# A one-core trunk layer on Trainium2: places of its own for the first half of a second operand set, a new order of vector work, one square on another engine, a last product over three steps

## The chip, the cores and the metric

The kernel runs on one NeuronCore of one Trainium2 chip. The metric is device time in microseconds (us). Engines: PE (TensorE, matrix products), DVE (VectorE), ACT (ScalarE), POOL (GpSimd), SP (SyncE, which issues DMAs), and 16 DMA engines. Each engine takes its own instructions strictly in program order; semaphores order one engine against another.

## The reference

One layer, with x of 1024 x 2048 and all in float32:

```python
hn = rmsnorm(x, norm_w)
proj = hn @ w_in                      # (1024, 2048) @ (2048, 6400)
q, k, v, g_attn, h, c_gate, b_gate, g_conv = split(proj)
attn = windowed attention(q, k, v)    # 16 query heads, 2 kv heads, bias, sinks
conv = b_gate * causal_conv3(c_gate * h)
mixed = concat(attn * silu(g_attn), conv * silu(g_conv))
x = x + mixed @ w_out                 # (1024, 2048) @ (2048, 2048)
return rmsnorm(x, final_norm_w)
```

## The kernel before

**Products.** The float32 products are made from halves: every operand is split into a high part (rounded to the type fp32r, by an ACT copy) and a low part (what is left, by a DVE subtraction), and a product is three matmuls (high x high, high x low, low x high). Each pair of 2 x 2 blocks is multiplied by Strassen's method in Winograd's form, so there are seven products per block (named 1 to 7 by `p`), each over 8 slices of the inner dimension, taken two slices to a step: four steps a product, 28 steps a block of output columns (`LEN`), eight blocks (`BLOCKS`: GATES, QKV, four convolution blocks, OUT0, OUT1), 224 steps in all (`STEPS`). A step is four output tiles (five in block QKV) of 6 matmuls each. The order of the products in block GATES is 2, 1, 3, 6, 7, 5, 4: steps 0 to 3 are product 2, steps 4 to 7 product 1, steps 8 to 11 product 3, and so on.

**What feeds a step n.** `w_hi(n)` (ACT, L947) and `w_lo(n)` (DVE, L1293) split two slices of weights from `raw` into a ring of three places. In the blocks GATES and OUT0 (`ON_CHIP`), `x_hi(l)` (ACT, L973) and `x_lo(l)` (DVE, L1301), l = 2n and 2n+1, split the activation side from `z` into five places of `x_main`; POOL then stores the halves to the DRAM tensor `x_park` (`store_x`, L488), and the blocks that follow load them from there (`load_x`, SP, L546). A place of `x_main` can be written again when its step is done and its store has landed. Some products take sums of blocks: `s1` to `s4` (DVE, L1355, L1361, L1373, L1367) make them in `raw` for weights, `t1` to `t4` in `z` for activations. `w_hi` of steps 8 to 11 waits for `s4`.

**The first block.** The input x arrives untransposed. PE turns it: first the left half (`turn_x0`, L1826), then, once ACT has scaled it by the row norms (`scale_x_lo`, `scale_x_hi`, L995, L999), the right half (`turn_x1`, L1862). DVE takes turned slices 0 to 7 of the right half straight into `t1` (`t1_from_turn`, L1332); ACT copies slices 8 to 15 (`place_1`, L1005). The first tile of step 8 waits for all eight copies (`wait_bank`). The row norms of the left half come from eight ACT squares (`square_x0`, L982), three small POOL operations (`x_inv_std`), a PE product that spreads them (`turn_factors`, L1842) and a DVE copy (L1656).

**Parking.** Steps 0 to 3 (product 2) ran on activations without the norm factor, so their halves are not the ones that later blocks need. `b21` (DVE, L1340) multiplies `z[:, 0, 8:16]` by the factors in place, `park_hi` (ACT) and `park_lo` (DVE, L1347) split each of its 8 slices again, and `store_park` (POOL, L845, L847) stores both halves, 16 stores of 256 KB. The loads of steps 28 to 31 wait until all have landed; the places of step 28's load (`x_far0`) are also read until step 25.

**What orders the work.** Nothing plans it: each engine walks over the steps and the four quarters of each step, and tables such as `T1_AT[(step, quarter)]` say what is put in at that point of the engine's own queue. A position is an order, not a time; time is set by the waits. Within a quarter DVE takes: sums of finished tiles, `place_0`, `x_lo`, `w_lo`, `t1_from_turn`, `s1` and so on, in the order of the code. ACT takes `x_hi`, `w_hi`, squares, scalings, `place_1`, `park_hi`.

**The end.** The last `TAIL` steps are done tile by tile: tile 0 over these steps, then tile 1, and so on. After each tile DVE subtracts it into `e`, ACT squares it, DVE and POOL make the norm, and ACT and DVE scale the rows and ACT and SP store them.

Of the kernel before, what the change touches and what calls it, by code (L numbers as in the profile page):

```python
# [9 lines left out]
ALU = mybir.AluOpType  # L10
# [56 lines left out]
XH = 5  # L67
TAIL = 2

# [93 lines left out]
def _slots():  # L163
    holder, loads, stores = {}, {}, {}
    for n in range(STEPS):
# [12 lines left out]
        else:  # L178
# [3 lines left out]
            for j in places:  # L182
# [33 lines left out]
W_LO_AT = {(1, 0): 2, (2, 1): 3, (2, 3): 4}  # L216
X_HI_AT = {(1, 0): (4,), (1, 1): (5,), (1, 3): (6,), (2, 0): (7,), (3, 2): (8, 9), (4, 0): (10,),
           (4, 1): (11,), (4, 3): (12,), (5, 0): (13,), (5, 1): (14,), (6, 0): (15,), (7, 1): (16,), (7, 2): (17,),
           (7, 3): (18,)}
X_LO_AT = {(1, 0): (4,), (1, 1): (5,), (1, 3): (6,), (2, 0): (7,), (3, 2): (8, 9), (4, 0): (10,),  # L220
           (4, 2): (11,), (4, 3): (12,), (5, 0): (13,), (5, 1): (14,), (6, 0): (15,), (7, 1): (16,), (7, 2): (17,),
           (7, 3): (18,)}
# [22 lines left out]
def build(nc, x, norm_w, w_in, sinks, conv_w, conv_b, w_out, rel_bias, final_norm_w, one_hot, out):  # L245
    ctx = ExitStack()
    with ctx:
# [38 lines left out]
        x_tile[7] = [place[:, 1, k:k + 2, :].rearrange("p a c -> p (a c)") for place, k in ((z, 4), (raw, 14))]  # L286
        square = z[:, 1, 0:2, :].rearrange("p a c -> p (a c)")
        setup_rows = scratch[0:(TAPS + 1) * GROUPS + KT, 0:P]
# [206 lines left out]
        def _(sp):  # L495
# [31 lines left out]
            def load_x(n):  # L527

                b, p, q = place(n)
                made = GATES if b < OUT0 else OUT0  # L530
                for was, i in X_BEFORE[n, 0]:
                    sp.wait_ge(step_done, was + 1)
                    if was // LEN in ON_CHIP:
                        sp.wait_ge(x_stored[was // LEN == OUT0][S_TURN[was, i][0]], S_TURN[was, i][1])
                if x_pair(n) > 1 and n - (made + 1) * LEN < 2:

                    sp.wait_ge(x_lo_ready, x_index(at(made, 4, QP - 1 if x_pair(n) == 3 else 1), 1) + 1)
                for i in range(2):
                    if is_parted(at(made, p, q)):
                        sp.wait_ge(park_stored, 16 * 2 * HK)  # L540
# [283 lines left out]
        def _(pool):  # L824
# [7 lines left out]
            def x_inv_std(tiles, turn):  # L832

                pool.wait_ge(x_squared, 8 + 2 * turn)
                pool.tensor_tensor(x_var[:, tiles], x_ssq[:, tiles], x_ssq_lo[:, tiles], ALU.add).then_inc(x_var_ready, 1)
                pool.wait_ge(x_var_ready, 2 * turn + 1)
                pool.tensor_scalar(x_var[:, tiles], x_var[:, tiles], 1.0 / D, EPS, ALU.mult, ALU.add
                                   ).then_inc(x_var_ready, 1)
                pool.wait_ge(x_var_ready, 2 * turn + 2)
                pool.tensor_tensor(x_rstd[:, tiles], x_var[:, tiles], minus_half[:, 0:tiles.stop - tiles.start], ALU.pow  # L840
                                   ).then_inc(x_rstd_ready, 1)

            def store_park(j):
                pool.wait_ge(park_hi_ready, j + 1)
                pool.dma_start(x_park[0, j // 2, :, j % 2, 0:N], z[:, 1, j, :]).then_inc(park_stored, 16)  # L845
                pool.wait_ge(park_lo_ready, j + 1)
                pool.dma_start(x_park[0, j // 2, :, j % 2, N:], z[:, 0, HK + j, :]).then_inc(park_stored, 16)  # L847
# [82 lines left out]
        def _(act):  # L930
# [54 lines left out]
            def square_x(t):  # L985
                i = TILES1.index(t)
                act.wait_ge(x_part_loaded[(1, 2, 0, 5)[t - 4]], 32 if t == 7 else 48)
                for c in range(2):
                    act.wait_ge(x_squared, 8 + 2 * i + c)
                    act.activation(square, x_tile[t][c], ACT.Square,  # L990
                                   accum_out=(x_ssq if c else x_ssq_lo)[:, t:t + 1]).then_inc(x_squared, 1)
# [16 lines left out]
            def park_hi(j):  # L1008

                act.wait_ge(b21_ready, j // 2 + 1)  # L1010
                act.wait_ge(x_lo_ready, x_index(at(GATES, 5, j // 2), j % 2) + 1)
                act.activation(z[:, 1, j, :].bitcast(F32R), z[:, 0, HK + j, :], ACT.Copy).then_inc(park_hi_ready, 1)

            def copy_out(b, p, t):

                to = (0, 2, 3)[COPIED[b].index(p)]
                if t == 0:
# [21 lines left out]
                    else:  # L1039
                        if b == GATES:  # L1040
                            act.wait_ge(x1_turned, KT)
                        elif b == QKV:
# [13 lines left out]
            def tanh_gate(i, half):  # L1056
# [4 lines left out]
                if i > 0:  # L1061
                    act.wait_ge(gate_stored[0], 16)
                else:
                    act.wait_ge(x1_turned, KT)
                if i > 1:
# [4 lines left out]
            def more_hi(p):  # L1070
                i = AT[QKV][p]
                c, h = W_HOME[p]
                if i == 0:

                    act.wait_ge(x_lo_ready, 2 * LEN)
                    act.wait_ge(park_stored, 16 * 2 * HK)
                if p == 2:
# [104 lines left out]
            for n in range(STEPS):  # L1182
                b, p, q = place(n)
                i = AT[b][p]
                for quarter in range(4):
# [23 lines left out]
                    if quarter == 0:  # L1209
                        l = 2 * n + 3  # L1210
                        if X_TABLED <= l < 2 * STEPS and l // (2 * LEN) in ON_CHIP:
                            x_hi(l // 2, l % 2)
                        if 5 <= n + 2 < STEPS:
                            w_hi(n + 2)
# [43 lines left out]
                    if b == OUT1:  # L1258
# [19 lines left out]
            square_y(20, 3, 0)  # L1278
            for t in range(4):
                if t < 3:  # L1280
                    square_y(21 + t, 3, t + 1)
                scale_back(0, t)
                store_back(0, t)
# [3 lines left out]
        def _(dve):  # L1287
# [16 lines left out]
            def place_0(k):  # L1304
# [38 lines left out]
            def park_lo(j):  # L1343

                dve.wait_ge(park_hi_ready, j + 1)
                dve.wait_ge(t4_ready, j // 2 + 1)
                dve.tensor_tensor(z[:, 0, HK + j, :].bitcast(F32R), z[:, 0, HK + j, :], z[:, 1, j, :], ALU.subtract  # L1347
                                  ).then_inc(park_lo_ready, 1)
# [293 lines left out]
            for n in range(STEPS):  # L1642
                b, p, q = place(n)
                i = AT[b][p]
                for quarter in range(4):
# [18 lines left out]
                    if (n, quarter) in W_LO_AT:  # L1664
                        w_lo(W_LO_AT[n, quarter])
                    if quarter == 0:
                        l = 2 * n + 3
# [14 lines left out]
                    if quarter == 1:  # L1682
                        if 5 <= n + 2 < STEPS:
                            w_lo(n + 2)
# [3 lines left out]
                    if b == GATES:  # L1688
                        for k in T1_AT.get((n, quarter), ()):
                            t1_from_turn(k)  # L1690
                        if quarter == 0 and 5 <= n < 9:
                            s1(GATES, n - 5)
                        if (n, quarter) in B21_AT:
# [5 lines left out]
                    if quarter == 2:  # L1699

                        if 5 <= n < 9:
                            s2(GATES, n - 5)
                            s4(GATES, n - 5)
                        wb, wp, wq = place(n + 2) if n + 2 < STEPS else (BLOCKS, 0, 0)
# [97 lines left out]
            for t in range(4):  # L1802
                sums(OUT1, 4, t)
                if t > 0:
                    finish_0(t - 1)
                y_variance(4 + t)
            finish_0(3)


        @block.tensor  # L1810
        def _(pe):
# [227 lines left out]
```

## Time and profile before

| | |
|---|---|
| median of 3 runs | 1361.8 us (1359.88 to 1362.35) |
| the profiled execution's own time | 1360.45 us |
| its span, first to last instruction | 1358.6 us |
| PE busy | 1335.0 us, 98% |
| DVE, ACT, POOL busy | 919.3, 538.6, 93.3 us |
| DMA over the span | 287 GB/s |

The times in rows are from the first instruction; about 1.85 us of the execution's own time lie outside the span. A row of a timeline gives start, duration, engine, line, operation, tiles out and in, shape and count, and in brackets how long the engine had been idle before it and what ended that. Ends of matmuls are modelled: the next matmul can start before the row's end.

### The profile page before, as it was taken

The numbers are of one execution on the slowest core, as the hardware profiler recorded it, in microseconds if no ns is written. First come the engines' busy times: TensorE is split into PE (matmuls) and PEld (weight loads), VectorE is DVE, ScalarE is ACT, GpSimd is POOL, SyncE is SP. The second block draws the span as 40 slices with busy tenths as digits, with TensorE's granted clock in tenths as the row PEclk, the third lists the DMA queues.
The fourth block names the chain that finished last, engine by engine and source line by source line (L and its number), as shares of the span: only waits on it lengthen the run. The fifth ranks groups of instructions, "written<-read, shape, count | busy, mean of one in ns | idle before, by whom it ended". The sixth has DMA issues, their size and how long they took to land.

```text
span 1358.6 us, 16600 instructions
## 1 busy us (share of the span) xinstructions
PE 1335.0 (98%) x6034; PEld 1102.0 (81%) x6034; DVE 919.3 (68%) x1141; ACT 538.6 (40%) x941; POOL 93.3 (7%) x158
## 2 busy tenths in 40 slices
PE   9899999999999999999999999999999999999997
PEld 7688878888887888888888888878888788888886
DVE  5888976423467557985589845898439896666376
ACT  6754532322233443434334343343423444421454
POOL 0211411000000000000000000000000221200001
PEclk9999999999999999999999999999999999999999
DMA  9766995988978999969999699987988888899777
GB/s 327 293 233 248 398 411 198 285 298 283 336 246 274 278 292 309 260 215 284 286 290 281 199 316 289 294 252 218 297 315 319 322 269 278 280 317 358 281 253 305
DMA packets 206432, 390.02 MB, mean 287 GB/s; under 512 B 78912, under 2 KB 129168, under 8 KB 184720
## 3 DMA queue, kind: packets, MB, share of 16 engines
q1 hardware_dynamic: 186768, 321.83, 72.4%
q0 software_dynamic: 18368, 62.92, 12.6%
q10 hardware_dynamic: 1216, 4.21, 0.8%
q8 instruction: 48, 0.79, 0.2%
q14 instruction: 32, 0.26, 0.1%
HBM read 294.18 MB, written 98.93 MB: 289 GB/s over the span
## 4 chain that ended last, share of the span: by engine, by line
PE 87%; DVE 5%; DMA 4%; issue 2%; ACT 1%; SPq 0%; POOL 0%; DVEq 0%; ACTq 0%; POOLq 0%
PE banks L1902 82%; DMA x_far<-x_park 1%; DMA x_park<-z 1%; PE banks L1925 1%; PE banks L1937 1%; DMA qkv_park<-e 1%; DVE w_ring L1293 1%; PE banks L1946 1%; DVE x_main L1301 1%; PE banks L1947 1%; DVE raw L1355 0%; PE banks L1826 0%; DVE e L1444 0%; DVE z L1400 0%; DMA raw<-in_w_in_dram 0%
## 5 line engine op out<-in xcount | busy, mean ns | idle before, releaser
L1902 PE MATMUL banks<-x_main,w_ring 128*128 128x512 f32 x2352 | 552.4, 392 | 0.4 <-ACT x_main L973 0.2
L1902 PEld LDWEIGHTS banks<-x_main,w_ring 128*128 128x128 f32 x2352 | 438.8, 188 | 90.8 <-issue 1.1
L947 ACT ACTIVATE w_ring<-raw 128x1024 fp32r<-128x1024 f32 x224 | 236.4, 1056 | 550.4 <-PE banks L1902 539.2
L1293 DVE TENSOR_TENSOR w_ring<-raw,w_ring 128x1024 fp32r<-128x1024 f32 x224 | 274.2, 1224 | 218.8 <-ACT w_ring L947 218.7
L1902 PE MATMUL banks<-x_far,w_ring 128*128 128x512 f32 x1680 | 395.2, 392 | 3.9 <-DMA x_far<-x_park 3.8
L1902 PEld LDWEIGHTS banks<-x_far,w_ring 128*128 128x128 f32 x1680 | 314.0, 188 | 69.5 <-issue 4.4
L1902 PE MATMUL banks<-w_ring,x_main 128*128 128x512 f32 x1008 | 230.0, 389 | 0.8 <-DVE x_main L1301 0.8
L1902 PEld LDWEIGHTS banks<-w_ring,x_main 128*128 128x128 f32 x1008 | 189.1, 188 | 40.5 <-issue 1.2
L488 POOL DMA_DIRECT2D x_park<-x_main x104 | 56.1, 540 | 1019.3 <-DVE x_main L1301 1014.5
L973 ACT ACTIVATE x_main<-z 128x512 fp32r<-128x512 f32 x112 | 69.8, 624 | 136.7 <-issue 94.5
L1301 DVE TENSOR_TENSOR x_main<-z,x_main 128x512 fp32r<-128x512 f32 x112 | 76.8, 688 | 47.6 <-ACT x_main L973 47.5
L1902 PE MATMUL banks<-w_ring,x_far 128*128 128x512 f32 x336 | 77.4, 389 | 0.1
L1902 PEld LDWEIGHTS banks<-w_ring,x_far 128*128 128x128 f32 x336 | 63.0, 188 | 13.5 <-issue 0.5
L1054 ACT ACTIVATE e<-banks 128x512 f32<-128x512 f32 x92 | 54.7, 597 | 46.3 <-PE banks L1902 45.8
L1107 ACT ACTIVATE probs<-logits,small 128x129 f32<-128x129 f32 x128 | 50.0, 393 | 47.1 <-DVE small L1510 47.0
L1498 DVE SCALAR_TENSOR_TENSOR logits<-banks,bias 128x512 f32<-128x512 f32 (+1 forms) x32 | 21.5, 672 | 45.8 <-PE banks L1925 45.8
L1361 DVE TENSOR_TENSOR raw<-raw 128x1024 f32<-128x1024 f32 x32 | 41.2, 1288 | 1.1
L1367 DVE TENSOR_TENSOR raw<-raw 128x1024 f32<-128x1024 f32 x32 | 39.2, 1224 | 2.9
L1373 DVE TENSOR_TENSOR raw<-raw 128x1024 f32<-128x1024 f32 x32 | 39.1, 1221 | 0.4
L1355 DVE TENSOR_TENSOR raw<-raw 128x1024 f32<-128x1024 f32 x32 | 39.0, 1218 | 0.0
L1434 DVE TENSOR_TENSOR e<-e,banks 128x512 f32<-128x512 f32 x24 | 16.4, 685 | 27.6 <-PE banks L1902 14.3
L1423 DVE TENSOR_TENSOR e<-e,banks 128x512 f32<-128x512 f32 x32 | 21.4, 684 | 19.0 <-PE banks L1902 18.9
(143 smaller groups left out, 855.1 us busy)
## 6 DMA issues: line engine op xcount, KB each, us to landing
x_far<-x_park SPq DMA_DIRECT2D x84, 1024.0 KB, 7.2
x_main<-x_park SPq DMA_DIRECT2D x84, 1024.0 KB, 7.1
x_park<-x_main POOLq DMA_DIRECT2D x104, 512.0 KB, 5.4
raw<-in_w_in_dram SPq DMA_DIRECT2D x128, 256.0 KB, 5.3
raw<-in_w_in_dram SPq DMA_DIRECT2D x32, 512.0 KB, 11.1
raw<-in_w_out_dram SPq DMA_DIRECT2D x32, 512.0 KB, 6.0
q_cur<-qkv_park SPq DMA_DIRECT2D x64, 128.0 KB, 5.5
z<-mix_park SPq DMA_DIRECT2D x16, 512.0 KB, 8.0
```

The costliest lines, as they stand in the source:

```text
L488: engine.dma_start(x_park[0 if n < LEN else 1, n % LEN, :, i, :], x_main[:, k, :, :].rearrange("p a c -> p (a c)").bitcast(F32)).then_inc( ...
L947: act.activation(w_ring[:, n % NW, :, 0, :], raw[:, c, k:k + 2, :], ACT.Copy).then_inc(w_hi_ready, 1)
L973: act.activation(x_halves(n)[i][:, 0, :], z[:, h, kt16, :], ACT.Copy).then_inc(x_hi_ready, 1)
L1054: act.activation(e_tile(b, to, t), banks[:, BANK[b, p, t], :], ACT.Copy).then_inc(copy_ready, 1)
L1107: op = act.activation(probs[:, j, :], logits[u % 2][:, j, :], ACT.Exp, bias=row_min[:, j:j + 1], scale=-1.0, accum_out=row_sum[:, j:j + 1])
L1293: dve.tensor_tensor(w_ring[:, n % NW, :, 1, :], raw[:, c, k:k + 2, :], w_ring[:, n % NW, :, 0, :], ALU.subtract).then_inc(w_lo_ready, 1)
L1301: dve.tensor_tensor(half[:, 1, :], z[:, h, k * HK + 2 * q + i, :], half[:, 0, :], ALU.subtract).then_inc(x_lo_ready, 1)
L1355: dve.tensor_tensor(raw[:, 1, k, :], raw[:, 1, k, :], raw[:, 1, high, :], ALU.add).then_inc(s1_ready, 1)
L1361: dve.tensor_tensor(raw[:, 0, k, :], raw[:, 1, k, :], raw[:, 0, k, :], ALU.subtract).then_inc(s2_ready, 1)
L1367: dve.tensor_tensor(raw[:, 0, high, :], raw[:, 0, high, :], raw[:, 0, k, :], ALU.subtract).then_inc(s4_ready, 1)
L1373: dve.tensor_tensor(raw[:, 0, k, :], raw[:, 1, high, :], raw[:, 0, k, :], ALU.subtract).then_inc(s3_ready, 1)
L1902: op = pe.matmul(bank, left, right, start=(first and i == 0), stop=(kt == HK - 1 and i == 2), skip_group_check=goes_on)
```

## The change

- `b21(0)` and `b21(1)` move from steps 16 and 17 to steps 10 and 13. The second splitting of slices 0 to 3 moves from steps 19 and 20 to steps 11, 15 and 16. It writes both halves into parts of `e` that are free then (`park_stage`), and POOL stores both with one DMA of 512 KB (4 stores in place of 8). ACT's first tanh waits for two of them, ACT's copies of product 7 for all four. The waits for 16 stores become waits for the 12.
- `s2`, `s4` of the first weight sums move from quarter (5, 2) to (6, 1), behind the first four `t1_from_turn`; the others from (6, 2), (7, 2) to (7, 1), (7, 3); `s1(1)` from (6, 0) to (7, 0), `s1(2)` from (7, 0) to (7, 2).
- `w_hi(7)` moves from (5, 0) to (5, 2), `w_hi(8)` from (6, 0) to (6, 1), `w_hi(9)` from (7, 0) to (7, 2), `w_lo(7)` from (5, 1) to (5, 3), `w_lo(8)` from (6, 1) to (7, 0), `w_lo(9)` from (7, 1) to (7, 3), `x_hi` and `x_lo` of l = 15 from (6, 0) to (5, 3). The four `scale_x_hi` move from (5, 2), (5, 3) to (6, 0).
- The square of row tile 3's low half goes from ACT to DVE, as a product and a reduction.
- `TAIL` is 3; a step's operands are waited for where its first tile uses them; DVE's `finish_0(t)` comes right behind `y_variance(4 + t)`, and ACT's squares at the end no longer run one tile ahead.

```diff
-TAIL = 2
+TAIL = 3
-              (2, 0): ((0, 0), (0, 1)), (2, 1): ((0, 2), (0, 3))}
+              (2, 0): ((0, 0), (0, 1)), (2, 1): ((0, 2),)}
+SQUARED_BY_DVE = (2, 2)
-SCALE_HI_AT = {(5, 2): (7, 4), (5, 3): (5, 6)}
+SCALE_HI_AT = {(6, 0): (7, 4, 5, 6)}
-W_HI_AT = {(1, 0): 2, (2, 0): 3, (2, 3): 4}
-W_LO_AT = {(1, 0): 2, (2, 1): 3, (2, 3): 4}
+W_HI_AT = {(1, 0): 2, (2, 0): 3, (2, 3): 4, (3, 0): 5, (4, 0): 6, (5, 2): 7, (6, 1): 8, (7, 2): 9}
+W_LO_AT = {(1, 0): 2, (2, 1): 3, (2, 3): 4, (3, 1): 5, (4, 1): 6, (5, 3): 7, (7, 0): 8, (7, 3): 9}
+W_TABLED = 10
+S1_AT = {(5, 0): 0, (7, 0): 1, (7, 2): 2, (8, 0): 3}
+S24_AT = {(6, 1): 0, (7, 1): 1, (7, 3): 2, (8, 2): 3}
-B21_AT = {(16, 3): 0, (17, 3): 1, (18, 3): 2, (19, 3): 3}
-PARK_AT = {(19 + j // 2, 1 + 2 * (j % 2)): j for j in range(HK)}
+B21_AT = {(10, 3): 0, (13, 3): 1, (18, 3): 2, (19, 3): 3}
+PARK_AT = {(11, 1): 0, (11, 3): 1, (15, 1): 2, (16, 1): 3, (21, 1): 4, (21, 3): 5, (22, 1): 6, (22, 3): 7}
+STAGED = 4
...
+        park_stage = [e[:, i, 2 * j:2 * j + 2, :] for i in (1, 3) for j in range(2)]
...
             def store_park(j):
+                if j < STAGED:
+                    if j == 2:
+                        pool.wait_ge(park_stored, 16 * 2)
+                    pool.wait_ge(park_lo_ready, j + 1)
+                    pool.dma_start(x_park[0, j // 2, :, j % 2, :], park_stage[j].rearrange("p a c -> p (a c)")
+                                   ).then_inc(park_stored, 16)
+                    return
+                if j == STAGED:
+                    pool.wait_ge(park_stored, 16 * STAGED)
...
+            def square_last_low():
+
+                for i in (3, 4):
+                    dve.wait_ge(x_part_loaded[i], 16)
+                dve.tensor_tensor(squares, x_cols[0][:, 3, :], x_cols[0][:, 3, :], ALU.mult).then_inc(cols_ready, 1)
+                dve.wait_ge(cols_ready, 3)
+                dve.tensor_reduce(x_ssq_lo[:, 3:4], squares, AX_X, ALU.add).then_inc(cols_ready, 1)
...
-            for n in range(STEPS - TAIL, STEPS):
-                wait_operands(n)
             for t in range(4):
                 for n in range(STEPS - TAIL, STEPS):
                     q = place(n)[2]
+                    if t == 0:
+                        wait_operands(n)
```

## Rows read from the trace of the kernel before

**Rows 1.** The page, busy time of the engines.
```profile
PE 1335.0 (98%) x6034; PEld 1102.0 (81%) x6034; DVE 919.3 (68%) x1141; ACT 538.6 (40%) x941; POOL 93.3 (7%) x158
```

**Rows 2.** Timeline of PE alone, first 200 us.
```profile
32.02 1.16 PE L1842 MATMUL banks<-ident,small 128*128 128x128 f32 x8 [1.11 <-POOL small L840]
...
44.29 0.63 PE L1826 MATMUL banks<-ident,z 128*128 128x128 f32 x4 [0.98 <-DVE z L1313]
...
53.20 0.55 PE L1862 MATMUL banks<-ident,e 128*128 128x128 f32 x3 [0.98 <-ACT e L995]
...
59.27 0.55 PE L1862 MATMUL banks<-ident,e 128*128 128x128 f32 x3 [1.36 <-DVE z L1332]
...
66.73 0.67 PE L1862 MATMUL banks<-ident,e 128*128 128x128 f32 x3 [2.08 <-DVE z L1332]
...
74.56 110.67 PE L1902 MATMUL banks<-x_main,w_ring 128*128 128x512 f32 x487
...
188.72 7.33 PE L1902 MATMUL banks<-x_far,w_ring 128*128 128x512 f32 x24 [2.37 <-DMA x_far<-x_park]
```

**Rows 3.** Windows: length, busy of PE, PEld, DVE, ACT, POOL, granted clock, DMA.
```profile
68.00:70.00 2.00, 2.00 (x8) 1.61 (x7) 1.69 (x2) 1.60 (x3) 0.00 (x0) 0.50 0.00 0
...
190.00:192.00 2.00, 2.00 (x6) 1.56 (x5) 2.00 (x4) 0.00 (x0) 0.00 (x0) 0.50 1.06 384
```

**Rows 4.** Timeline of ACT, the last of the eight squares of the left half.
```profile
29.05 1.06 ACT L982 ACTIVATE z<-z 128x1024 f32<-128x1024 f32 x1
```

**Rows 5.** Groups by shape on DVE: busy us, mean ns.
```profile
L1510 DVE TENSOR_REDUCE small<-logits 128x4 f32<-128x516 f32 x32 | 22.1, 691 | 1.1
```

**Rows 6.** Timeline of DVE, steps 2 to 7.
```profile
31.18 1.23 DVE L1293 TENSOR_TENSOR w_ring<-raw,w_ring 128x1024 fp32r<-128x1024 f32 x1 [4.55 <-ACT w_ring L947]
...
53.88 1.22 DVE L1361 TENSOR_TENSOR raw<-raw 128x1024 f32<-128x1024 f32 x1
55.20 1.23 DVE L1367 TENSOR_TENSOR raw<-raw 128x1024 f32<-128x1024 f32 x1
57.86 0.69 DVE L1301 TENSOR_TENSOR x_main<-z,x_main 128x512 fp32r<-128x512 f32 x1 [1.43 <-ACT x_main L973]
58.47 2.72 DVE L1332 SCALAR_TENSOR_TENSOR z<-banks,cols,z 128x512 f32<-128x512 f32 x4
```

**Rows 7.** Timeline of ACT, steps 5 to 7.
```profile
49.50 1.04 ACT L947 ACTIVATE w_ring<-raw 128x1024 fp32r<-128x1024 f32 x1
...
65.95 1.06 ACT L947 ACTIVATE w_ring<-raw 128x1024 fp32r<-128x1024 f32 x1 [7.18 <-DVE raw L1367]
...
75.13 1.26 ACT L1005 ACTIVATE z<-banks,cols 128x512 f32<-128x512 f32 x2
```

**Rows 8.** Chain of waits, 155 to 200 us.
```profile
159.98 14.92 DMA x_park<-z
...
174.98 13.64 DMA x_far<-x_park
```

**Rows 9.** DMA queues (packets, MB, share) and issues (to landing), 142 to 162 us.
```profile
q0 software_dynamic: 1540, 5.37, 66.0%
...
raw<-in_w_in_dram SPq DMA_DIRECT2D x4, 512.0 KB, 21.8
```

**Rows 10.** Timelines of ACT, DVE and POOL before step 28.
```profile
178.86 0.63 ACT L973 ACTIVATE x_main<-z 128x512 fp32r<-128x512 f32 x1 [1.25 <-DMA x_park<-x_main]
...
181.62 3.44 DVE L1451 SCALAR_TENSOR_TENSOR e<-e 128x1024 f32<-128x1024 f32 x1
...
187.25 1.21 DVE L1458 TENSOR_TENSOR xw<-x_raw,xw 128x1024 fp32r<-128x1024 f32 x1
...
181.07 2.91 POOL L855 TENSOR_TENSOR x_raw<-x_raw 128x1024 f32<-128x1024 f32 x1
```

**Rows 11.** Timeline of all engines, the end.
```profile
1350.01 0.69 DVE L1444 TENSOR_TENSOR e<-e,banks 128x512 f32<-128x512 f32 x1 [0.72 <-PE banks L1902]
...
1352.96 1.15 ACT L1161 ACTIVATE raw<-raw,small 128x1024 f32<-128x1024 f32 x1 [0.47 <-POOL small L883]
```

More of the change, by code:

```diff
@@ L286, in build @@
         x_tile[7] = [place[:, 1, k:k + 2, :].rearrange("p a c -> p (a c)") for place, k in ((z, 4), (raw, 14))]
-        square = z[:, 1, 0:2, :].rearrange("p a c -> p (a c)")
+        square, squares = (z[:, 1, k:k + 2, :].rearrange("p a c -> p (a c)") for k in (0, 2))
+        park_stage = [e[:, i, 2 * j:2 * j + 2, :] for i in (1, 3) for j in range(2)]
         setup_rows = scratch[0:(TAPS + 1) * GROUPS + KT, 0:P]
@@ L539, in load_x @@
                     if is_parted(at(made, p, q)):
-                        sp.wait_ge(park_stored, 16 * 2 * HK)
+                        sp.wait_ge(park_stored, 16 * (2 * HK - STAGED))
                     else:
@@ L832, in x_inv_std @@
             def x_inv_std(tiles, turn):
-                pool.wait_ge(x_squared, 8 + 2 * turn)
+                pool.wait_ge(x_squared, 7 + 2 * turn)
+                pool.wait_ge(cols_ready, 4)
                 pool.tensor_tensor(x_var[:, tiles], x_ssq[:, tiles], x_ssq_lo[:, tiles], ALU.add).then_inc(x_var_ready, 1)
@@ L988, in square_x @@
                 for c in range(2):
-                    act.wait_ge(x_squared, 8 + 2 * i + c)
+                    act.wait_ge(x_squared, 7 + 2 * i + c)
                     act.activation(square, x_tile[t][c], ACT.Square,
@@ L1010, in park_hi @@
                 act.wait_ge(b21_ready, j // 2 + 1)
+                if j < STAGED:
+                    act.wait_ge(x1_turned, KT)
+                    act.activation(park_stage[j][:, 0, :].bitcast(F32R), z[:, 0, HK + j, :], ACT.Copy
+                                   ).then_inc(park_hi_ready, 1)
+                    return
                 act.wait_ge(x_lo_ready, x_index(at(GATES, 5, j // 2), j % 2) + 1)
@@ L1040, in copy_out @@
                         if b == GATES:
-                            act.wait_ge(x1_turned, KT)
+                            act.wait_ge(park_stored, 16 * STAGED)
                         elif b == QKV:
@@ L1063, in tanh_gate @@
                 else:
-                    act.wait_ge(x1_turned, KT)
+                    act.wait_ge(park_stored, 16 * 2)
                 if i > 1:
@@ L1075, in more_hi @@
                     act.wait_ge(x_lo_ready, 2 * LEN)
-                    act.wait_ge(park_stored, 16 * 2 * HK)
+                    act.wait_ge(park_stored, 16 * (2 * HK - STAGED))
                 if p == 2:
@@ L1212, in _ @@
                             x_hi(l // 2, l % 2)
-                        if 5 <= n + 2 < STEPS:
+                        if W_TABLED <= n + 2 < STEPS:
                             w_hi(n + 2)
@@ L1277, in _ @@
                             store_back(1, 2 * quarter - 3)
-            square_y(20, 3, 0)
             for t in range(4):
-                if t < 3:
-                    square_y(21 + t, 3, t + 1)
+                square_y(20 + t, 3, t)
                 scale_back(0, t)
@@ L1345, in park_lo @@
                 dve.wait_ge(park_hi_ready, j + 1)
+                if j < STAGED:
+                    dve.tensor_tensor(park_stage[j][:, 1, :].bitcast(F32R), z[:, 0, HK + j, :], park_stage[j][:, 0, :],
+                                      ALU.subtract).then_inc(park_lo_ready, 1)
+                    return
                 dve.wait_ge(t4_ready, j // 2 + 1)
@@ L1665, in _ @@
                         w_lo(W_LO_AT[n, quarter])
+                    if (n, quarter) == SQUARED_BY_DVE:
+                        square_last_low()
                     if quarter == 0:
@@ L1682, in _ @@
                     if quarter == 1:
-                        if 5 <= n + 2 < STEPS:
+                        if W_TABLED <= n + 2 < STEPS:
                             w_lo(n + 2)
@@ L1690, in _ @@
                             t1_from_turn(k)
-                        if quarter == 0 and 5 <= n < 9:
-                            s1(GATES, n - 5)
+                        if (n, quarter) in S1_AT:
+                            s1(GATES, S1_AT[n, quarter])
+                        if (n, quarter) in S24_AT:
+                            s2(GATES, S24_AT[n, quarter])
+                            s4(GATES, S24_AT[n, quarter])
                         if (n, quarter) in B21_AT:
@@ L1699, in _ @@
                     if quarter == 2:
-                        if 5 <= n < 9:
-                            s2(GATES, n - 5)
-                            s4(GATES, n - 5)
                         wb, wp, wq = place(n + 2) if n + 2 < STEPS else (BLOCKS, 0, 0)
@@ L1803, in _ @@
                 sums(OUT1, 4, t)
-                if t > 0:
-                    finish_0(t - 1)
                 y_variance(4 + t)
-            finish_0(3)
+                finish_0(t)
         @block.tensor
```

4 lines of the change are left out of this document (2 added, 2 removed).

## The prediction, made before the change was run

> **What bounds the kernel now.** I read the page's busy times first: PE is busy 98% of the span and no other engine over 68% [rows 1]. So the floor is PE's own work, which the change leaves as it is, and only what keeps PE idle or slow can be won. PE's timeline, read for its brackets, shows where that is: from 74.56 us it runs 487 products in 110.67 us without a gap, 0.2272 us a product, 1.36 us a tile, 5.45 us a step of 24 [rows 2]. Before that it stops for 1.11 us (the norm factors), 0.98 (a turned slice not yet taken by DVE), 0.98 (ACT's scaling), 1.36 and 2.08 (DVE's T1), and at 186.4 for 2.37 (step 28's load) [rows 2]. Start to start each stop costs some 0.15 us more than its bracket, as the modelled ends reach past the next start. Behind the two longest stops the windows show the granted clock at 0.50, its lower level of 1.2 GHz [rows 3]; behind those of 1.36 us and less it stayed at 2.4 GHz. From the start of the first product behind each, I count 1.65 us lost to it: step 28 takes 8.5 us where step 29 takes 6.8, and a tile of step 7 takes 2.5 where the next takes 1.36. Last, the chain of waits shows what released step 28: a park store 14.92 us in flight, then the load, 13.64 us [rows 8].
>
> **Part 1, the square.** The last of ACT's eight squares goes; they follow each other every 1.26 us [rows 4], so ACT is done that much sooner. On DVE the product costs 1.22 us, as other two-operand instructions of 128 x 1024 [rows 6]. No row has a reduction of 1024 elements: 516 take 0.69 us [rows 5], so it is over 0.69 and, if all of it scaled, 1.38; I take 1.25, since most of it should scale. DVE lies idle 4.55 us up to 31.18 [rows 6], thus from 26.6, and the sum is there at 26.6 + 1.2 + 0.1 + 1.25 = 29.1, just behind ACT at 28.95. POOL's three operations begin at 29.2 in place of 30.35 and PE goes on at 30.86 in place of 32.02, where step 3's first tile ends at 30.76. Gain 1.15 us; with the reduction at either bound 1.25 to 1.0. DVE's chain from there (factors, places, splits) moves with it, so the stop at 44.29 [rows 2] stays and only moves.
>
> **Part 2, scaling.** `w_hi(7)`, 1.04 us (0.95 to the next start) [rows 7], stands ahead of two of the four scalings that the stop at 53.20 waits for, and goes behind them. ACT is otherwise without a gap there, so the stop falls from 0.98 to about 0.05: 1.1 us start to start. All slots that `w_hi(7)` and `x(15)` want are free when they come; they are not late for step 7.
>
> **Part 3, T1 first.** The stop at 59.27 ends when DVE's first T1 does. It was behind `s2`, `s4` (53.88 to 56.4) and behind `x_lo(15)`, which waited for ACT's four scalings (1.43 us idle up to 57.86) [rows 6]. Now PE turns slices 0 to 3 from 51.1 to 52.8. DVE has ahead of T1 only `x_lo(15)` (52.55) and `w_lo(7)` (1.14), so the four T1, 0.66 us apart [rows 6], run from 54.3 to 57.0. PE comes back for slice 4 at 55.65 and finds the first done at 55.03; the fourth is 0.1 late. Gain 1.5 for the stop and 0.4 since PE's four turns there were paced by DVE. Then `s2`, `s4` (1.32 + 1.14) and four T1 end at 62.0, the first of them at 60.13, as PE arrives at 60.3: the stop of 2.08 goes too (2.25 start to start), less 0.1, and with it the half clock of 1.65. So PE is ready for step 8 at about 77.4 - 1.15 - 1.1 - 1.9 - 2.15 - 1.65 = 69.45.
>
> **Part 3, its price.** The sums of weights do not vanish, they queue up. From 62.0 DVE has `w_lo(8)` 1.14, `s1(1)` 1.13, a sum of tiles 0.6, `x_lo(16)` 0.6, `s2(1)` 1.32 and `s4(1)` 1.22: 68.0. `w_hi(9)` waits for that `s4`, as it did before (7.18 us idle up to 65.95) [rows 7], but now it stands in ACT's queue ahead of four of the eight `place_1` that step 8 waits for. Behind 68.0 ACT needs 0.95 + two copies 1.2 + `x_hi(18)` 0.52 + two copies 1.26 [rows 7] = 3.95: 72.0. So I expect a new stop of 2.5 us ahead of step 8, released by ACT's `place_1`. It is longer than the 2.08 that was followed by the lower clock [rows 2, 3], and I take it that it is again. Next, DVE: from 68.0 up to and with `x_lo(21)`, which step 10 needs, it has three single sums and four `x_lo` (4.3), `s1` twice (2.3), two `w_lo` (2.3), two pairs `s2`, `s4` (4.9), `t2(0)` (1.14) and a last end: 83.45. PE arrives at 72.0 + 10.9 = 82.95 with the full clock, at 84.0 to 84.6 with the lower one. Step 10 began at 74.56 + 60 x 0.2272 = 88.2 before [rows 2], and now at 84.5: the early part is worth 3.7 us, 4.7 if the clock stays up. The ends for this price: no new stop at all (6.5 us won in place of 3.7), or all of DVE's delay twice over (1.2 won).
>
> **Part 4, parking early.** `b21(0)`, `b21(1)` and four splits are 1.14 and 0.6 each on DVE; steps 10 to 16 have 3.5 to 4.6 us of other DVE work in 5.45 us, save step 15 with 7.0, and what is over there is made up in step 16, so PE waits for none. The last parks stand where they stood, and ACT's `x_hi(47)` ahead of them waits for PE's step 21 as before: DVE being lighter alone brings 0.3 us. What counts is the queue. POOL's DMA queue moved 5.37 MB in the 20 us from 142 to 162, 0.27 MB/us, while the DMA engines were full with the other queue's traffic [rows 9]. Of what it held, 2.1 MB go to steps 11 to 16. That brings its later stores forward by 2.1 / 0.27 = 7.8 us; at the whole DMA rate of 405 GB/s there it would be 5.2. I take 6.5. The last park lands at 168.4 in place of 174.9 (times of the old frame), the load of step 28 is then held by SP's earlier weight load to 169.4, 5.6 us ahead of 174.98 [rows 8], and even if it still takes 13.64 us it lands at 183.0, ahead of 186.4. Next late is DVE: `x_hi(55)` waited for a store until 178.86, and its chain ends with `xw` at 188.46, only 0.26 ahead of PE's 188.72 [rows 2, 10]. That store now lands ahead of step 25's end at 175.48, so the chain begins 3.4 us sooner and ends at 185.1, ahead of PE. So the 2.37 us and their clock go: 2.5 + 1.65 = 4.15. Bounds: nothing, and 4.15.
>
> One row in that chain is long: a DVE instruction of 3.44 us where its like take 1.2, begun 0.55 us behind a POOL addition of 2.91 us [rows 10]; it ends 1.1 us behind POOL's end, so it stood still until POOL was done. The Trainium skill says why ("SBUF — State Buffer", section "SBUF: two separate sides"): DVE with two SBUF inputs and GpSimd share a port pair under an exclusive lock, held for a whole instruction. The trace agrees. It speaks against this change: POOL's addition follows the store of `x(55)` and so comes sooner together with the chain; by the rule the chain stays 8.9 us long and PE has 1.3 us in hand, without it 6.6 and 3.6 in hand.
>
> **Part 5, the end.** A tile now takes three steps' 18 products, 4.1 us in place of 2.7, so when the last ends no work of tile 2 is left. Before, ACT's last scaling began 2.95 us behind DVE's last subtraction, behind another scaling and a DMA issue, and DVE's variance stood behind `finish_0(2)` [rows 11]. The bare chain (subtraction 0.7, square 0.75, variance 0.4, POOL 0.6) is 2.5: 0.45 us won; nothing to 0.6 as bounds. Step 223's weights are wanted at 1336.2, 2.7 us sooner; they are ready at 1336.07. If they are late, tile 0 is, and it costs that much.
>
> **Sum.** 3.7 + 4.15 + 0.45 = 8.3. The profiled execution took 1360.45, so 1352.15 by its own time. The median of the runs lies 1.35 above it; I add part of that: 1352.7.
>
> **Rivals.** (a) DVE's queue in steps 6 to 10 is later than reckoned, because cross-engine waits add to each item: ten more handovers of 0.2 us make the early part 1.7, and the time 1354.7. For it: in steps 6 to 9 DVE has no idle time left in my plan. Against: the old rows hold such waits already. (b) Step 28 still waits: the loads there share full DMA engines and had 13 to 15 us in flight, and DVE's chain has 1.3 us in hand. Only a third of 4.15 comes, 1355.5; if nothing, 1356.9. Against: two independent estimates of the store queue clear it. (c) Slower: ACT's copies of product 7 (step 19, some 15 us behind the fourth staged store's issue) now wait for all four staged stores, and its first tanh for two; ACT is in order and feeds every step. Each us that the stores land beyond 15 + 5 us then stops PE one for one; it decides beyond 28 us in flight (20 + 8.3). SP's weight loads had 21.8 us in the median at 142 to 162 [rows 9], but steps 11 to 16 lie ahead of that stretch. At 32 us: 1365. (d) The time won early comes back, since DMA traffic of the full stretch at 136 to 188 is the bound and is only met 4 us sooner: 1360.5, no change. Against: 2.1 MB have left that stretch, and 4 us are worth 1.6 MB.
>
> **Chances.** Forecast (its own range 1350.3 to 1354.3, the upper clock within it) 0.62; (a) 0.16; (b) 0.13; (c) 0.04; (d) 0.05. A measurement of this kernel tells a change from none beyond about 0.2%, 2.7 us. Faster: 0.62 + 0.16 + 0.13 = 0.91 and 0.01 of (d); same 0.04; slower 0.04. The range takes in (a) and most of (b): 1349.8 to 1357.0.
>
> **What would show it.** Right: in PE's timeline no stops by DVE T1 or ACT's scaling over 0.3 us in steps 6 and 7, one new stop of some 2.5 us by ACT L1005's successor ahead of step 8, step 10 at 83.5 to 84.7; step 28 without a stop and at the full clock; the last park in flight under 10 us; the time from PE's last product to the span's end 8.2 in place of 8.65. Wrong: a stop by `x_lo` or `w_lo` in steps 9 to 19, any by ACT's copies at step 19, or step 28 released by DMA or by `xw`.

## The result

The changed kernel takes 1351.88 us in the median of 4 runs (1350.50 to 1352.58) against 1362.07 for the kernel before beside it: a ratio of 0.9925, 95% interval 0.9908 to 0.9942. In two later sets it stood at 0.9940 (0.9927 to 0.9952) and 0.9940 (0.9921 to 0.9960). Forecast were 1352.7 us, 1349.8 to 1357.0. The profiled execution took 1350.50 us with a span of 1348.7, against 1360.45 and 1358.6: 9.9 us less, where the sum said 8.3.

The page of the changed kernel, first part; it answers to [rows 1]:

```profile
PE 1331.5 (99%) x6034; PEld 1099.8 (82%) x6034; DVE 921.0 (68%) x1143; ACT 537.9 (40%) x939; POOL 91.0 (7%) x154
```

PE has 3.5 us less of busy time although it does the same products: a matmul at the lower clock counts as a longer one, and the two stretches at the lower clock are gone. PE's timeline, which answers to [rows 2] (L1857 is the old L1826, L1893 the old L1862, L1933 the old L1902):

```profile
30.82 1.16 PE L1873 MATMUL banks<-ident,small 128*128 128x128 f32 x8
...
43.09 0.63 PE L1857 MATMUL banks<-ident,z 128*128 128x128 f32 x4 [0.97 <-DVE z L1332]
...
51.05 0.55 PE L1893 MATMUL banks<-ident,e 128*128 128x128 f32 x3
...
55.63 0.49 PE L1893 MATMUL banks<-ident,e 128*128 128x128 f32 x3
...
60.24 0.51 PE L1893 MATMUL banks<-ident,e 128*128 128x128 f32 x3
...
72.12 8.21 PE L1933 MATMUL banks<-x_main,w_ring 128*128 128x512 f32 x35 [2.51 <-DVE x_main L1320]
...
181.64 5.60 PE L1933 MATMUL banks<-x_far,w_ring 128*128 128x512 f32 x24
```

The brackets of four rows are gone; the forecast starts were 30.86, 51.1, 55.65 and 60.3. The new bracket of 2.51 us ahead of step 8 stands where it was forecast, at 72.12 for 72.0, though it names DVE and not ACT (more on that below). Only the clock behind it is otherwise. Windows of the changed kernel (columns as in [rows 3]), over the stop and the first products behind it:

```profile
70.00:72.00 2.00, 0.00 (x0) 0.00 (x0) 2.00 (x4) 2.00 (x5) 0.20 (x2) 1.00 0.74 299
72.00:74.00 2.00, 1.88 (x8) 1.60 (x9) 1.90 (x3) 0.43 (x1) 0.35 (x1) 1.00 0.59 221
```

So the gain of the two profiles, by places. I count the starts of the tiles' products, 24 to a step and 30 in block QKV. Step 10 begins at 83.55 in place of 88.28: 4.73 us. From there to step 30 it is 111.69 in place of 115.80: 4.11. Behind the first products of attention, at 400 us, a stop for a load has 0.58 us in place of 1.44: 0.86. From PE's last product to the span's end it is 8.29 in place of 8.67: 0.38. That makes 10.1; some 0.1 us was lost in small pieces elsewhere. The row of that stop, in the kernel before and in the changed one:

```profile
410.80 3.41 PE L1902 MATMUL banks<-x_far,w_ring 128*128 128x512 f32 x14 [1.44 <-DMA x_far<-x_park]
...
401.11 3.21 PE L1933 MATMUL banks<-x_far,w_ring 128*128 128x512 f32 x13 [0.58 <-DMA x_far<-x_park]
```

The 0.86 is no merit of the change but luck of this profile: in two more profiles of the same kernel that stop has 1.6 and 1.7 us.

### The profile page after: what moved, and what is told of

Its sections match the earlier page's. It is cut to its first block, busy times and chain, and to the rows that moved or that the text cites. A ratio compares the mean times of both kernels' runs of the same rounds, so it can differ in the third digit from the quotient of the medians.

```text
span 1348.7 us, 16598 instructions
## 1 busy us (share of the span) xinstructions
PE 1331.5 (99%) x6034; PEld 1099.8 (82%) x6034; DVE 921.0 (68%) x1143; ACT 537.9 (40%) x939; POOL 91.0 (7%) x154
## 4 chain that ended last, share of the span: by engine, by line
PE 88%; DVE 6%; issue 3%; DMA 2%; ACT 1%; SPq 0%; POOL 0%; DVEq 0%; ACTq 0%; POOLq 0%
PE banks L1933 85%; PE banks L1956 1%; PE banks L1968 1%; DVE w_ring L1312 1%; DMA qkv_park<-e 1%; PE banks L1977 1%; DVE raw L1386 1%; PE banks L1978 1%; DVE x_main L1320 0%; DVE raw L1392 0%; DVE e L1475 0%; PE banks L1857 0%; DMA x_far<-x_park 0%; DVE z L1359 0%; DMA raw<-in_w_in_dram 0%
## 5 line engine op out<-in xcount | busy, mean ns | idle before, releaser
L1933 PE MATMUL banks<-x_main,w_ring 128*128 128x512 f32 x2352 | 552.2, 392 | 3.2 <-DVE x_main L1320 2.8
L1933 PEld LDWEIGHTS banks<-x_main,w_ring 128*128 128x128 f32 x2352 | 437.8, 188 | 94.3 <-issue 4.8
L1933 PE MATMUL banks<-x_far,w_ring 128*128 128x512 f32 x1680 | 393.5, 391 | 0.7 <-DMA x_far<-x_park 0.6
L1933 PEld LDWEIGHTS banks<-x_far,w_ring 128*128 128x128 f32 x1680 | 313.0, 188 | 65.5 <-issue 0.8
L1933 PE MATMUL banks<-w_ring,x_main 128*128 128x512 f32 x1008 | 230.6, 389 | 0.8 <-DVE x_main L1320 0.8
L1933 PEld LDWEIGHTS banks<-w_ring,x_main 128*128 128x128 f32 x1008 | 189.1, 188 | 40.6 <-issue 1.2
L1933 PE MATMUL banks<-w_ring,x_far 128*128 128x512 f32 x336 | 77.9, 390 | 0.0
L1933 PEld LDWEIGHTS banks<-w_ring,x_far 128*128 128x128 f32 x336 | 63.0, 188 | 13.4 <-issue 0.4
```

The source lines that it names most:

```text
L1933: op = pe.matmul(bank, left, right, start=(first and i == 0), stop=(kt == HK - 1 and i == 2), skip_group_check=goes_on)
```

## The experiments

**The changed kernel twice more.** No edit.

> The changed kernel as it is, beside the others of this call. All theories: 1351 to 1353 us, step 8 behind a stop of about 2.5 us, step 10 at about 83.5, no stop at step 28. Open is the clock: if a stop of that length brings the lower clock in some executions and not in others, this profile may show it at 0.5 behind step 8, and the time is about 1 us more; if it never does, as in the first profile, steps 8 and 9 take 5.45 us each.

> The changed kernel once more, as the measure for the run with the held loads: 1351 to 1353 us. Both theories: step 10 near 83.5 if the clock stays up behind the stop ahead of step 8, 84.5 if not.

Measured: 1351.69 us (5 runs) and 1354.03 us (6 runs, 1351.16 to 1355.92). The second median lies 1 us above the expected range; the kernel before stood higher beside it too, 1361.85 against 1360.13, and the ratio is 0.9940 both times. The first again has the full clock behind the stop. In the second it fell; its windows:

```profile
70.00:72.00 2.00, 0.00 (x0) 0.00 (x0) 2.00 (x4) 2.00 (x5) 0.20 (x2) 1.00 0.78 314
72.00:74.00 2.00, 1.76 (x5) 1.41 (x6) 1.91 (x2) 0.55 (x2) 0.47 (x1) 0.60 0.52 201
```

Step 8 then lasts 7.2 us in place of 5.6 and step 10 begins at 84.84, 1.3 us later than in the first profile (0.1 of it from ahead of the stop). The stop is 2.5 us in both. The forecast's 84.5 is this case.

**Late parks.** Everything of the change but the parking; ACT's waits for the staged stores go with it (not shown):

```diff
-B21_AT = {(10, 3): 0, (13, 3): 1, (18, 3): 2, (19, 3): 3}
-PARK_AT = {(11, 1): 0, (11, 3): 1, (15, 1): 2, (16, 1): 3, (21, 1): 4, ...
-STAGED = 4
+B21_AT = {(16, 3): 0, (17, 3): 1, (18, 3): 2, (19, 3): 3}
+PARK_AT = {(19 + j // 2, 1 + 2 * (j % 2)): j for j in range(HK)}
+STAGED = 0
```

> Everything of the change but the parking, which is where it was before (16 stores in steps 19 to 22). Theory (the stores' queue holds back step 28's load): the last park is 14 to 15 us in flight, step 28 begins behind a stop of 2.4 us or more released by the load, with the lower clock behind it: 4.1 us more than the changed kernel. Second theory (the DMA traffic of 136 to 188 us is the bound, and its end stays nearly where it is in absolute time): the stop is longer, up to 7 us, and the early gain is lost: 7 to 8 us more. Rival (DVE's chain was what held step 28): no stop by DMA, under 1 us more.

Measured: 1359.08 us, ratio 0.9987 (0.9978 to 0.9997), some 7 us more than the changed kernel beside it. Its chain of waits, and PE's row behind it:

```profile
156.42 15.00 DMA x_park<-z
...
171.49 16.30 DMA x_far<-x_park
```

```profile
187.88 7.70 PE L1933 MATMUL banks<-x_far,w_ring 128*128 128x512 f32 x24 [5.07 <-DMA x_far<-x_park]
```

Against [rows 8]: the last park leaves 3.6 us sooner than in the kernel before and is as long in flight, but the load then takes 16.3 us in place of 13.64 and lands only 0.8 us sooner. The second theory holds: step 10 begins 3.5 us sooner than in the kernel before and step 30 only 0.5. What PE wins early, it waits away at step 28, and the clock fell behind the stop there and behind the one at step 8 too.

**The two halves, each without the other.** The early parking alone: old tables of steps 5 to 9, square on ACT, `TAIL` 2. The new order alone: these with the tables of steps 5 to 9 new and the parks late.

> The kernel before with the early parking alone. All theories: step 28 reached at 186.4 as before. Theory (traffic ahead of the load is the bound, 2.1 MB of it gone to where there was room): the last park lands 2 to 4 us sooner than 174.9, the load at 183 to 186, no stop and no lower clock at step 28: 4.1 us less. Rival (DVE's chain up to xw is next): a stop of 0.3 to 2 us there, released by DVE, and 2 to 3.5 us less.

> The new order of steps 5 to 9 alone: square on ACT, parks late, the last product over two steps. Additive theory: step 10 at 84.7, 3.6 us ahead of before, and that stays: 3.6 us less. Theory after the run with the late parks (step 28's load lands at 188 whatever PE does before): step 28 is reached at 182.8, waits until 188, and starts at most 1 us sooner than the 188.72 of before; with one half-clock stretch behind either stop at most 1.5 us less in all.

Measured: parking alone 1357.70 us, ratio 0.9966 (0.9954 to 0.9979); order alone 1359.19 us, 0.9982 (0.9970 to 0.9994). PE's rows at step 28, first with the parking alone:

```profile
186.54 5.60 PE L1936 MATMUL banks<-x_far,w_ring 128*128 128x512 f32 x24
```

and with the order alone:

```profile
187.15 5.69 PE L1936 MATMUL banks<-x_far,w_ring 128*128 128x512 f32 x24 [3.22 <-DMA x_far<-x_park]
...
194.98 5.27 PE L1936 MATMUL banks<-x_far,w_ring 128*128 128x512 f32 x22 [0.79 <-DMA x_far<-x_park]
```

The parking alone clears the stop and its clock: the last park lands at 172.35, 2.6 us sooner than in the kernel before, and the load at 183.92, 4.7 us sooner, both as expected. The order alone reaches step 28 at 183.8 and must wait for a load that lands at 187.06. It did better than the 1.5 us at most that were expected: step 28 begins 1.6 us sooner than in the kernel before and not 1.0, and the clock stayed up behind the stop. So the 2.4 us that step 10 was ahead of the kernel before are still 2.2 at step 30.

The halves are worth 4.6 us (0.34%) and 2.5 us (0.18%) alone. Everything but the parking, the run above, is worth 1.8 us (0.13%); with the parking it is 8 to 10 us (0.60 to 0.75%), more than the 0.47% of the two added. The intervals are too wide for the medians alone to show that surplus. The rows show it: without the parking PE stops 3.2 and 5.1 us at step 28; in the changed kernel and with the parking alone it does not.

**The old order.** The changed kernel with the old tables of steps 5 to 9:

> The changed kernel with the old order of steps 5 to 9 (square on DVE, parks early, last product over three steps kept). Additive: the factors' stop gone (1.15), all other early stops back, of 1.0, 1.4 and 2.1 us, with the lower clock behind the last; step 10 at 87.1, step 28 at 185.2 without a stop; 3.6 us more than the changed kernel. Rival (the later end of the early part is hidden by some stop further on): less than 2 us more.

Measured: 1355.77 us, ratio 0.9955 (0.9938 to 0.9972). Its early stops are back; timeline of PE:

```profile
52.45 0.55 PE L1893 MATMUL banks<-ident,e 128*128 128x128 f32 x3 [0.98 <-ACT e L1011]
...
58.53 0.55 PE L1893 MATMUL banks<-ident,e 128*128 128x128 f32 x3 [1.36 <-DVE z L1359]
...
65.99 0.52 PE L1893 MATMUL banks<-ident,e 128*128 128x128 f32 x3 [2.07 <-DVE z L1359]
```

Here the clock stayed at 1.00 behind the 2.07, which in [rows 2, 3] it did not. So step 10 begins at 86.09, a us sooner than expected. Between this profile and the changed kernel's first, step 10 and step 28 both differ by 2.5 us, and that is what the order is worth with the clock up in both. By the ratios it is 2 to 4 us (0.9955 against 0.9940 and 0.9925), with intervals that overlap, so the 3.6 us expected are neither shown nor refuted.

**Which gate at steps 8 to 10.** `w_hi(9)` alone behind the copies:

```diff
-... (6, 1): 8, (7, 2): 9}
+... (6, 1): 8, (8, 0): 9}
```

> Only w_hi(9) goes behind all eight copies that step 8 waits for. Theory (DVE's queue up to x_lo(21) is the gate of step 10): the stop of 2.5 us ahead of step 8 is gone, and two others take its place, 1.4 us ahead of step 9 for x_lo(19) and 1.7 us ahead of step 10 for x_lo(21); step 10 at 83.5 as in the changed kernel, the time the same within 0.2 us. Rival (ACT's queue is the gate): step 10 at 81 and 2.5 us less in all.

Measured: 1351.25 us, ratio 0.9941 (0.9921 to 0.9960), as the changed kernel. PE's timeline:

```profile
66.57 8.47 PE L1933 MATMUL banks<-x_main,w_ring 128*128 128x512 f32 x36
...
76.43 5.72 PE L1933 MATMUL banks<-x_main,w_ring 128*128 128x512 f32 x24 [1.39 <-DVE x_main L1320]
83.50 6.86 PE L1933 MATMUL banks<-x_main,w_ring 128*128 128x512 f32 x29 [1.35 <-DVE x_main L1320]
```

The stop ahead of step 8 is gone: the step begins at 69.41. No instruction of DVE moved; the `x_lo` next to the old stop ran from 70.84 in the changed kernel and from 70.80 here. So the stop was ACT's, whatever the bracket of the changed kernel names. Step 10 begins at 83.50 all the same. DVE's queue up to `x_lo(21)` is the gate, and the 2.51 us in front of it cost nothing beyond the clock that may fall.

**Sums of weights behind the splits**, to relieve that queue; on top of the last one:

```diff
-S24_AT = {(6, 1): 0, (7, 1): 1, (7, 3): 2, (8, 2): 3}
+S24_AT = {(6, 1): 0, (7, 1): 1, (8, 0): 2, (9, 0): 3}
...
-                        late = 1 if b == GATES else 0     # t2
+                        late = 2 if b == GATES else 0
```

> w_hi(9) behind all eight copies, s2/s4 of slices 2 and 3 behind x_lo(19) and x_lo(21), t2 one step later. Theory (two gates in a row, ACT's copies at step 8 and DVE's queue at steps 9 and 10): both gone, step 8 at 69.5, step 10 at 80.4, step 11 at 86.8, held there a little by DVE, and steps 12 to 28 each 2.3 us ahead of the changed kernel: 2.3 us less in all. Rival (the DVE work itself is the bound, order doesn't matter): step 11 or 12 where it is in the changed kernel, and no gain. Second rival: step 28 waits again by the 2.3 us, since its load landed only 0.4 us ahead: no gain in all, with a stop of about 2 us there.

Measured: 1353.08 us, ratio 0.9948 (0.9935 to 0.9960), against 0.9940 for the changed kernel beside it: no gain, and within the intervals no sure loss. My reckoning was wrong and the first rival's sign is there: step 10 begins at 81.81, 1.7 us ahead of the changed kernel, and step 12 at 94.49, where it was. DVE's timeline:

```profile
79.23 1.23 DVE L1312 TENSOR_TENSOR w_ring<-raw,w_ring 128x1024 fp32r<-128x1024 f32 x1 [1.13 <-ACT w_ring L963]
...
85.25 1.23 DVE L1312 TENSOR_TENSOR w_ring<-raw,w_ring 128x1024 fp32r<-128x1024 f32 x1 [1.13 <-ACT w_ring L963]
```

With `s4` right ahead of the `w_lo` that needs it, DVE waits until ACT has made the high half in between: 1.13 us idle, twice, in a queue that had none. PE stopped 1.44 us ahead of step 11, and 1.16 in step 16 for DVE's sums of tiles, which put step 17 1.7 us behind the changed kernel's.

**A lighter queue.** `w_hi(9)` behind the copies, `t2` one step later, and of the parking `b21(1)` at (16, 0), parks 2 and 3 at (16, 2) and (17, 1).

> w_hi(9) behind the eight copies; the t2 one step later, which takes one DVE instruction of 1.14 us out of the queue ahead of x_lo(21) and ties no engine to another; b21(1) and parks 2 and 3 one to three steps later, out of DVE's queue ahead of the sums that step 16 waits for. Theory (from 52 to 122 us DVE has no idle time in the changed kernel, so PE is ahead only by what work is taken from DVE's queue): step 9 at 76.4, step 10 at 82.4 in place of 83.55, and steps 11 to 28 all 1.1 us ahead; 1.1 us less in all. Rival (steps 11 to 16 give it back, as where the sums of weights were moved): step 12 or 17 where it is in the changed kernel, no gain.

Measured: 1352.49 us, ratio 0.9937 (0.9917 to 0.9957), no better than the changed kernel. The profiled execution was its slowest, 1357.98 us; step 8 begins 2.0 us late in it from pieces in the first 13 us. Step 10 begins 12.96 us after step 8 (71.44, 84.40); with only `w_hi(9)` moved it was 14.09 (69.41, 83.50): the one instruction of 1.14 us is won. Then, at step 28:

```profile
187.02 7.07 PE L1933 MATMUL banks<-x_far,w_ring 128*128 128x512 f32 x24 [4.44 <-DMA x_far<-x_park]
```

The load was in flight for 17.28 us, against 13.8, 11.3 and 10.4 in the three profiles of the changed kernel. In this execution the gain came back as a stop four times as long, and the clock fell behind it, so that step 28 took 8.3 us. The load was not alone in being late; a weight load ahead of it held DVE, so that `xw`, which step 28 waits for too, ended only at 185.43:

```profile
181.93 1.23 DVE L1386 TENSOR_TENSOR raw<-raw 128x1024 f32<-128x1024 f32 x1 [3.96 <-DMA raw<-in_w_in_dram]
```

Why the transfers of this execution were so slow is not shown.

**Held loads.** On top of the lighter queue, SP issues three weight loads of block QKV later: one behind the load of step 28, two behind that of step 29 as well:

```diff
                         elif p == 5:
-                            load_raw(b + 1, 1, q)
+                            if b > GATES or q == 0:
+                                load_raw(b + 1, 1, q)
...
+                if n == 25:
+                    load_raw(QKV, 1, 1)
+                if n == 26:
+                    load_raw(QKV, 1, 2)
+                    load_raw(QKV, 1, 3)
```

> The lighter queue with three weight loads of block QKV (512 KB each, on SP's queue ahead of step 28's load, and not wanted by DVE until 182 us and later) moved behind the loads of steps 28 and 29. Theory (the traffic ahead of step 28's load holds it, 1.5 MB of it gone at 0.4 MB/us): the last park lands 1 to 2 us sooner, step 28's load 3 to 5 us sooner than in the lighter queue, no stop there in any execution; step 28 begins 1.1 us sooner than in the changed kernel: about 1.1 us less in all, 1350.5. Rival (the load is slow of itself, or the stores' queue alone counts): it still takes 11 to 17 us in flight, the stop at step 28 comes and goes as in the lighter queue, no gain. Second rival: DVE, in order, waits for a held load at 182 to 190 and takes PE with it: 1 to 4 us more.

Measured: 1351.51 us (1350.05 to 1355.03, 6 runs), ratio 0.9930 (0.9910 to 0.9951), with the changed kernel at 0.9940 beside it. Step 10 begins at 82.52, for the 82.4 that the lighter queue was to have. The last park lands at 165.44, 1.8 us sooner than with the lighter queue. Step 28's load lands at 176.71, 4.5 us sooner than in the changed kernel's first profile (2.3 and 3.2 in the other two), and PE's row is

```profile
180.52 5.60 PE L1939 MATMUL banks<-x_far,w_ring 128*128 128x512 f32 x24
```

1.1 us sooner, as expected. But the second rival came true in part: DVE, in order, waited for a held load, and PE for DVE.

```profile
184.41 1.22 DVE L1392 TENSOR_TENSOR raw<-raw 128x1024 f32<-128x1024 f32 x1 [2.60 <-DMA raw<-in_w_in_dram]
...
186.29 1.66 PE L1939 MATMUL banks<-x_far,xw 128*128 128x512 f32 x6 [0.17 <-DVE e L1481]
```

Step 28 takes 7.26 us in place of 6.80, and of the 1.1 us 0.65 are left at step 29. The intervals overlap: whether this version is faster, these runs can't tell.

**The square and the end, one each.** Back on ACT; `TAIL` 2 with the old order of finishing. One run each, so the times tell little and the rows are what counts.

> Only the square back on ACT. Theory: the stop by POOL ahead of the factors is back (1.1 us), everything up to step 28 is 1.15 us later, and so is the end. Rival (DVE's chain starts from the factors, but step 10 is held by DVE's later queue, which begins with ACT's scaling): the 1.15 us are made up by step 10.

> Only the end as before, two steps a tile and the old order of finishing. Theory: from PE's last product to the span's end 8.65 us in place of 8.3, 0.35 to 0.45 us; nothing else changes. Rival (three steps a tile make PE wait for step 223's weights in the changed kernel): PE's own last three steps are shorter here by 0.1 us or more.

Measured: with the square on ACT the second tile of step 3 begins at 32.81 in place of 31.73, step 10 at 84.61 in place of 83.55, step 28 at 182.72 in place of 181.64: 1.1 us at every point, 1352.19 us in all. With two steps a tile the last product ends at 1341.28 and the span at 1350.1: 8.8 us in place of 8.29. The last three steps themselves take 16.48 in place of 16.53 us. The four profiles with the old end have 8.67 to 8.89 us, the ten with the new one 8.28 or 8.29. So the end is worth 0.4 to 0.6 us.

## Why the prediction was right, point by point

**Part 1, the square:** right. DVE did it from 26.51 to 28.98, and the reduction, which no row had, took 1.22 us for 1.25 reckoned. Its worth is 1.1 us, shown by undoing it. Timeline of DVE, changed kernel:

```profile
27.76 1.22 DVE L1341 TENSOR_REDUCE small<-z 128x1 f32<-128x1024 f32 x1
...
66.77 1.23 DVE L1398 TENSOR_TENSOR raw<-raw 128x1024 f32<-128x1024 f32 x1
...
82.72 0.69 DVE L1320 TENSOR_TENSOR x_main<-z,x_main 128x512 fp32r<-128x512 f32 x1
```

**Parts 2 and 3:** right to 0.1 us, since engines with strict queues and known durations could be walked through. `s4(1)` ended at 68.00 for 68.0 reckoned, and `x_lo(21)` at 83.41 for 83.45. ACT, same kernel:

```profile
68.03 1.06 ACT L963 ACTIVATE w_ring<-raw 128x1024 fp32r<-128x1024 f32 x1 [2.86 <-DVE raw L1398]
68.99 1.25 ACT L1021 ACTIVATE z<-banks,cols 128x512 f32<-128x512 f32 x2
...
70.65 1.26 ACT L1021 ACTIVATE z<-banks,cols 128x512 f32<-128x512 f32 x2
```

What I had not seen is that the new stop is of no weight of its own, as DVE's queue would have stopped PE for the same time a little later. So my upper end for this part, 6.5 us won with no new stop at all, was wrong: with `w_hi(9)` moved there is none, and 4.8 us are won.

**The clock:** the one wrong term, 1.0 us. I took it that a stop of 2.5 us brings the lower clock because one of 2.08 had. Of the seven profiles with the stop of 2.5 us ahead of step 8, it fell behind it in four (the third of the changed kernel, late parks, order alone, `TAIL` 2) and not in three (the first two of the changed kernel, square on ACT). Behind the stop of 2.07 of the old order it fell with the parking alone and did not in the changed kernel with the old order. It is a chance to be put in with a weight; length alone does not settle it. That the first profile kept the clock was luck.

**Part 4, the parks:** the stop went, at the value reckoned (4.11 for 4.15), but by a wrong estimate. I said the last park would be 6.5 us sooner, in flight for under 10 us. It was in flight 12.3 us (155.12 to 167.40, two more profiles 12.2 and 13.1), 2.6 us less than in [rows 8]. The queues of the changed kernel in the same 20 us of its own frame (137.3 to 157.3) as [rows 9] show what became of the room:

```profile
q1 hardware_dynamic: 3578, 3.80, 53.6%
q0 software_dynamic: 1180, 4.18, 51.7%
...
raw<-in_w_in_dram SPq DMA_DIRECT2D x4, 512.0 KB, 18.9
```

POOL's queue had fewer bytes and moved them more slowly, 4.18 MB for 5.37, and the room went to SP's queue, whose weight loads were 18.9 us in flight in place of 21.8. The two together moved 8.0 MB where it had been 8.1: what one queue gave up, the other took. The held loads show it the other way: with SP's loads held the same 20 us have 3.15 MB on SP's queue and 4.77 on POOL's. I had divided the bytes taken away by one queue's rate, as if that rate were its own. SP then issued the load at 167.47, as the last park landed, and it landed at 181.24, 0.4 us ahead of PE's 181.64. I had counted on 3.4 us; the two more profiles have 2.9 and 3.3. So the load, in flight for 10.4 to 13.8 us, landed from 0.4 to 3.3 us ahead of need, and part of the success is luck: rival (b) was nearer than its 0.13, and in the one profile of the lighter queue, with an early gain 1.1 us larger, it came true. DVE's chain was as reckoned: `xw` ended at 180.6, 1.0 us ahead of PE (1.3 forecast). Its long instruction is there too, 3.43 us; it ended 1.1 us behind POOL's addition, as in the kernel before.

**Part 5, the end:** 0.38 us between the profiles for 0.45, 0.5 when undone. The last scaling began 2.48 us behind the last subtraction, 2.5 reckoned; rows of the changed kernel's timeline, which answer to [rows 11]:

```profile
1340.45 0.69 DVE L1475 TENSOR_TENSOR e<-e,banks 128x512 f32<-128x512 f32 x1 [0.36 <-PE banks L1933]
...
1342.93 1.15 ACT L1182 ACTIVATE raw<-raw,small 128x1024 f32<-128x1024 f32 x1 [1.04 <-POOL small L899]
```

**The rivals.** (a), more handovers than reckoned: no sign of it. (c), ACT held by the staged stores: they were in flight 4.8 to 7.4 us, and no stop at step 19. (d), the traffic takes the gain back: false for this change, true for all of it but the parking (0.13% left), and only in part for the order alone (0.18%).

**The total.** The sum had 1352.15 for the profiled execution and it took 1350.50. Of the 1.65 us between them the clock has 0.95 and the stop at 400 us, by luck, 0.86; small pieces took some 0.15 back. The median lies 1.4 us above the profiled execution, where I had added 0.55; that the forecast of the median is off by only 0.8 us owes something to these two errors of opposite sign. By the ratio of the two later sets, 0.9940, the change is worth 8.2 us, and I had forecast 9.1 between the medians.

## What to carry to other kernels

Where engines take their queues in order and all durations stand in the trace, walk every queue through the new order, with each handover, up to the point where all of them have caught up; that gave starts right to 0.1 us, and it shows which of two stops is the gate. Where the DMA engines are full, bytes taken from one queue do not free that queue alone, as here the other queue took the room: reckon with the bytes of all queues ahead of the transfer. A gain ahead of such a transfer is kept only as far as the traffic leaves room, so it should be made together with moving bytes away.

## What the runs showed of the hardware that I had not expected

The lower clock (1.2 GHz) behind a stop is not fixed by the stop's length. After the first 13 us the fourteen profiles have fifteen stops of PE of 2.07 to 5.07 us; it fell at nine of them, and at none of the shorter ones (up to 1.87 us). It fell at 2.07, 2.08, 2.37, 2.5, 4.44 and 5.07 us, and stayed up at other stops of 2.07 and 2.5, and at 2.65 and 3.22. Where it fell at step 8, that step took 7.1 to 7.2 us in place of 5.5 and step 10 began 1.1 to 1.2 us later; where it fell at step 28, that step took 8.3 to 8.9 us in place of 6.8. It may be a part of why runs of the same kernel lie 2 to 5 us apart; that was not tested. One 1 MB load behind the same queues took 10.4 to 13.8 us in flight in three executions of the same kernel, and 17.3 in one of its near kin. And a bracket in PE's timeline can name the wrong engine: `x_lo` was named for a wait that the moving of one ACT instruction removed.
